# Modulation and gate products on four 32-column groups of TensorE, and a new order of work around the first value tiles

## What is computed

```python
def ada_terms(c, w_ada, b_ada):              # c: 2 rows in all, w_ada: 1024 x 3072
    m = jax.nn.silu(c) @ w_ada + b_ada
    shift, scale, gate = jnp.split(m, 3, axis=-1)

def project(x, c, norm_g, w_ada, b_ada, w_in, b_f):
    h = rmsnorm(x, norm_g) * (1.0 + scale[:, None, :]) + shift[:, None, :]
    p = h @ w_in                             # 1024 -> q, k, v, ag, logf, u, pg
    ...
def merge(x, attn, ag, pool, pg, gate, w_out):
    z = jnp.concatenate([attn * jax.nn.silu(ag), pool * jax.nn.silu(pg)], axis=-1)
    return x + gate[:, None, :] * (z @ w_out)
```

## Time and profile before

| | us |
|---|---|
| median of three runs | 1312.25 |
| the profiled execution, its own time | 1314.26 |
| its span in the trace | 1312.5 |
| PE busy | 1265.6 (96%) |
| DVE, ACT, POOL busy | 712.4, 564.3, 180.5 |

### The profile page before, as it was taken

How to read it: one execution, slowest core, us unless ns; L and a number is a source line. 1 busy time by engine, 2 the same in 40 slices (tenths; PEclk the granted TensorE clock), 3 DMA queues, 4 the chain that set the end, 5 groups by cost and what they waited for, 6 DMA issues and landing times. The chain is left out here.

```text
span 1312.5 us, 19345 instructions
## 1 busy us (share of the span) xinstructions
PE 1265.6 (96%) x7007; PEld 1038.7 (79%) x7007; DVE 712.4 (54%) x1965; ACT 564.3 (43%) x1158; POOL 180.5 (14%) x193
## 2 busy tenths in 40 slices
PE   7899999999999999999969999999999998999997
PEld 1669988888888888888848777877877876788885
DVE  0636631344456221110029999999999989544444
ACT  2536531221121212111128887887878878111111
POOL 1223310100100010100000031122104105100000
PEclk9899999999999999999979999999999999999999
DMA  9636444221221443432148849968786986766662
GB/s 367 244 121 190 157 142 140 77 89 42 67 88 43 135 145 125 140 117 83 49 135 162 117 77 169 129 116 147 85 149 116 128 169 158 208 204 193 192 193 64
DMA packets 163836, 179.51 MB, mean 137 GB/s; under 512 B 35361, under 2 KB 125013, under 8 KB 159974
## 3 DMA queue, kind: packets, MB, share of 16 engines
q1 hardware_dynamic: 158478, 160.42, 49.5%
q10 hardware_dynamic: 5264, 17.86, 4.2%
HBM read 111.55 MB, written 66.69 MB: 136 GB/s over the span
## 5 line engine op out<-in xcount | busy, mean ns | idle before, releaser
L597 PE MATMUL prj_acc<-prj_hhi,til_whi 128*128 128x512 f32 (+1 forms) x800 | 286.4, 358 | 0.0
L598 PE MATMUL prj_acc<-prj_hhi,til_wlo 128*128 128x512 f32 (+1 forms) x800 | 284.2, 355 | 0.0
L599 PE MATMUL prj_acc<-prj_hlo,til_whi 128*128 128x512 f32 (+1 forms) x800 | 284.2, 355 | 0.0
L1588 DVE TENSOR_SCALAR_CACHE_REDUCE att_wts<-att_sps 128x512 f32<-128x512 f32 (+4 forms) x328 | 186.3, 596 | 105.3 <-PE att_sps L1475 99.9
L1598 DVE TENSOR_TENSOR att_wlo<-att_tps,att_whi 128x512 fp32r<-128x512 f32 (+1 forms) x336 | 183.1, 583 | 20.8 <-ACT att_whi L1551 20.1
L1551 ACT ACTIVATE att_whi<-att_tps 128x512 fp32r<-128x512 f32 (+1 forms) x336 | 161.5, 515 | 57.7 <-PE att_tps L1488 25.4
L1545 ACT ACTIVATE att_wts<-att_wts,att_nm 128x1024 f32<-128x1024 f32 (+8 forms) x200 | 175.2, 880 | 20.4 <-DVE att_nm L1593 18.6
L1488 PE MATMUL att_tps<-keep_ident,att_wts 128*128 128x128 f32 x1088 | 159.0, 277 | 9.8 <-DVE att_wlo L1598 7.7
L599 PEld LDWEIGHTS prj_acc<-prj_hlo,til_whi 128*128 128x128 f32 x800 | 150.8, 188 | 21.3
L597 PEld LDWEIGHTS prj_acc<-prj_hhi,til_whi 128*128 128x128 f32 x800 | 150.8, 188 | 21.0
L598 PEld LDWEIGHTS prj_acc<-prj_hhi,til_wlo 128*128 128x128 f32 x800 | 150.8, 188 | 20.8
(11 more groups left out here) (181 smaller groups left out, 1857.0 us busy)
## 6 DMA issues: line engine op xcount, KB each, us to landing
til_wraw<-in_w_in SPq DMA_DIRECT2D x20, 512.0 KB, 4.3
scratch_v<-val_vs SPq DMA_DIRECT2D x17, 512.0 KB, 4.7
val_xt<-in_x_prompt ACTq DMA_DIRECT2D x16, 512.0 KB, 4.4
ini_al<-in_w_ada SPq DMA_DIRECT2D x8, 1024.0 KB, 15.8
zin_zh<-scratch_z SPq DMA_DIRECT2D x16, 512.0 KB, 4.3
zin_zl<-scratch_z SPq DMA_DIRECT2D x16, 512.0 KB, 5.8
zin_xr<-in_x_prompt SPq DMA_DIRECT2D x16, 512.0 KB, 5.4
out_y_prompt<-zin_o ACTq DMA_DIRECT2D x16, 512.0 KB, 2.7
```

The source lines that it names most:

```text
L597: pe.matmul(out, w[0][:, k, :], hhi[:, k, cs], start=(k == 0), stop=False)
L598: pe.matmul(out, w[1][:, k, :], hhi[:, k, cs], start=False, stop=False)
L599: mm = pe.matmul(out, w[0][:, k, :], hlo[:, k, cs], start=False, stop=(k == KT - 1))
L1588: dve.tensor_scalar(weights(st, x.row, x.w0, x.n), sps[x.i % S_RING][0:x.m, 0:x.n], 1.0, None, ALU.mult, ALU.max, accum_out=top[0:x.m, e, ...
```

## The change

Four things are done.

1. The four products of a slab go to different 32-column groups of PE's array: the output of block n lies on PSUM partitions 32n and 32n + 1 instead of 0 and 1 (`QUAD`), still one bank for each n. The gate's columns are cut into four blocks of 256 with k outside, and go to the four groups in the same way. The rows that are made of them (`mrow`, `gate_b`, `grow`) lie on the same partitions; the gate's bias comes in four DMAs instead of one and the gate leaves in four.
2. turn(0) and turn(1) stand between the slabs, after slab 4 and slab 6, instead of around the turning of `mrow`.
3. On ACT, square(3) and root(3), the copies of `mrow` and norm(2) stand ahead of the rounding of the value weights, and high(0) after its first half. On DVE, stats(3) stands ahead of the copies, and the low halves of the value weights after modulate(0). The value weights are loaded to other columns of `ah`, so SP waits for `turned` ahead of them.
4. value(t) runs through all k-blocks of high x high, then of high x low, then of low x high, and waits for the low half of the rows only ahead of the third; for tile 0 it waits for the weights block by block.

```diff
-        vraw = ah[:, :, 0:VC]
-        mrow = al[0:2, 0, 0:2 * D]
-        grow = ah[0:2, 0, D:2 * D]
+        vraw = ah[:, :, D - VC:D]
+        QUAD = [slice(32 * n, 32 * n + 2) for n in range(4)]
+        mrow = [al[QUAD[n], 0, n * 512:(n + 1) * 512] for n in range(4)]
+        grow = [ah[QUAD[n], 0, D + n * 256:D + (n + 1) * 256] for n in range(4)]
...
                 sp.dma_start(slab[:, k, :], wada[:, k, 0:2 * D]).then_inc(ada_in[k], 16)
+            sp.wait_ge(turned, 1)
...
             def gate():
-                for n in range(2):
-                    for k in range(KT):
-                        mm = pe.matmul(xps[GATE_SLOT][0:2, n * 512:(n + 1) * 512], pair[:, k, :], graw[:, k, n * 512:(n + 1) * 512],
+                for k in range(KT):
+                    for n in range(4):
+                        cs = slice(n * 256, (n + 1) * 256)
+                        mm = pe.matmul(xps[GATE_SLOT][QUAD[n], cs], pair[:, k, :], graw[:, k, cs],
                                        start=(k == 0), stop=(k == KT - 1))
...
             def value(t):
-                pe.wait_ge(lo_ok, t + 1)
+                pe.wait_ge(hi_ok, t + 1)
...
-                for k in range(KT):
-                    if t == 0:
-                        pe.wait_ge(w_lo, k + 1)
-                    for h, w in ((hhi, vhi_w), (hhi, vlo_w), (hlo, vhi_w)):
+                for h, w, split in ((hhi, vhi_w, w_hi), (hhi, vlo_w, w_lo), (hlo, vhi_w, w_lo)):
+                    if h is hlo:
+                        pe.wait_ge(lo_ok, t + 1)
+                    for k in range(KT):
+                        if t == 0:
+                            pe.wait_ge(split, k + 1 if h is hhi else KT)
...
                 for n in range(4):
-                    mm = pe.matmul(ada[n][0:2, :], pair[:, k, :], slab[:, k, n * 512:(n + 1) * 512],
+                    mm = pe.matmul(ada[n][QUAD[n], :], pair[:, k, :], slab[:, k, n * 512:(n + 1) * 512],
                                    start=(k == 0), stop=(k == KT - 1))
+                if k in (4, 6):
+                    turn((k - 4) // 2)
             mm.then_inc(m_full, 1)
-            turn(0)
             pe.wait_ge(m_row, 4)
...
-            turn(1)
...
-            square(2)
-            root(2)
+            for t in range(2, 4):
+                square(t)
+                root(t)
+            act.wait_ge(m_full, 1)
+            for n in range(2):
+                act.activation(mrow[n], ada[n][QUAD[n], :], ACT.Copy).then_inc(m_row, 1)
+            norm(2)
             for k in range(KT):
                 if k % 4 == 0:
                     act.wait_ge(vw_in[k // 4], 48)
+                if k == 4:
+                    high(0)
                 act.activation(vhi_w[:, k, :], vraw[:, k, :], ACT.Copy).then_inc(w_hi, 1)
-            act.wait_ge(m_full, 1)
-            for n in range(2):
-                act.activation(mrow[:, n * 512:(n + 1) * 512], ada[n][0:2, :], ACT.Copy).then_inc(m_row, 1)
-            norm(2)
-            square(3)
-            root(3)
-            high(0)
```

More of the change, by code:

```diff
@@ L268, in stage_project @@
         graw = ah[:, :, D:2 * D]
-        vraw = ah[:, :, 0:VC]
-        mrow = al[0:2, 0, 0:2 * D]
-        grow = ah[0:2, 0, D:2 * D]
-        gate_b = al[0:2, 1, D:2 * D]
+        vraw = ah[:, :, D - VC:D]
+        QUAD = [slice(32 * n, 32 * n + 2) for n in range(4)]
+        mrow = [al[QUAD[n], 0, n * 512:(n + 1) * 512] for n in range(4)]
+        grow = [ah[QUAD[n], 0, D + n * 256:D + (n + 1) * 256] for n in range(4)]
+        gate_b = [al[QUAD[n], 1, D + n * 256:D + (n + 1) * 256] for n in range(4)]
         pair = sc[:, :].rearrange("p (w k) -> p k w", w=2)
@@ L410, in _ @@
             sp.wait_ge(m_full, 1)
-            sp.dma_start(gate_b, io["b_ada"][:, 2 * D:].partition_broadcast(2)).then_inc(gb_in, 16)
+            for n in range(4):
+                bias = io["b_ada"][:, 2 * D + n * 256:2 * D + (n + 1) * 256]
+                sp.dma_start(gate_b[n], bias.partition_broadcast(2)).then_inc(gb_in, 16)
             b = v_slot(-1)
@@ L416, in _ @@
                 if t == GATE_AT:
-                    sp.wait_ge(g_ok, 2)
-                    sp.dma_start(dram["gate"][:, :], grow).then_inc(g_out, 16)
+                    for n in range(4):
+                        sp.wait_ge(g_ok, n + 1)
+                        sp.dma_start(dram["gate"][:, n * 256:(n + 1) * 256], grow[n]).then_inc(g_out, 16)
                 if t == NT - 2:
@@ L477, in _ @@
             store_chunk(sp, TILE_CHUNKS[-1])
-            sp.wait_ge(g_out, 16)
+            sp.wait_ge(g_out, 64)
             sp.wait_ge(f_out, 16 * 22)
@@ L524, in turn @@
                 elif t == GATE_AT + 3:
-                    pe.wait_ge(g_ok, 2)
+                    pe.wait_ge(g_ok, 4)
                 elif t >= 2:
@@ L680, in high @@
                 if t == KT:
-                    act.wait_ge(g_out, 16)
+                    act.wait_ge(g_out, 64)
                 act.activation(hhi[:, :, t * P:t * P + n], hf[:, t % 2, :].rearrange("p (k c) -> p k c", k=KT)[:, :, 0:n],
@@ L884, in _ @@
             dve.tensor_scalar(one_b[:, :], cols[:, ROW_B + KT:ROW_B + 2 * KT], 1.0, None, ALU.add).then_inc(ab, 1)
-            stats(0)
-            stats(1)
-            stats(2)
+            for t in range(4):
+                stats(t)
+            dve.wait_ge(m_full, 1)
+            for n in range(2, 4):
+                dve.tensor_copy(mrow[n], ada[n][QUAD[n], :]).then_inc(m_row, 1)
+            dve.wait_ge(ab, 1)
+            dve.wait_ge(m_col, 1)
+            wide = [P, KT, 2]
+            for n, (dst, bias) in enumerate(((keep["scale"], one_b[:, :]), (keep["shift"], cols[:, ROW_B:ROW_B + KT]))):
+                for q in range(2):
+                    ks = slice(4 * q, 4 * q + 4)
+                    dve.tensor_tensor(dst[:, ks, :], ada[2 - 2 * n + q][:, 0:KT].rearrange("p (k w) -> p k w", w=2),
+                                      bias[:, ks].unsqueeze(2).broadcast_to([P, 4, 2]), ALU.add).then_inc(ab, 1)
+            dve.wait_ge(ab, 5)
+            dve.tensor_tensor(keep["scale"][:, :, :], keep["scale"][:, :, :],
+                              cols[:, ROW_G:ROW_G + KT].unsqueeze(2).broadcast_to(wide), ALU.mult).then_inc(ab, 1)
+            dve.wait_ge(ab, 6)
+            modulate(0)
             for k in range(KT):
@@ L890, in _ @@
                 dve.tensor_tensor(vlo_w[:, k, :], vraw[:, k, :], raw(vhi_w[:, k, :]), ALU.subtract).then_inc(w_lo, 1)
[L891 to L906, removed]
             modulate(1)
@@ L913, in _ @@
                     dve.wait_ge(g_full, 1)
[L914 to L917, removed]
+                    dve.wait_ge(gb_in, 64)
+                    for n in range(4):
+                        dve.tensor_tensor(grow[n], xps[GATE_SLOT][QUAD[n], n * 256:(n + 1) * 256], gate_b[n], ALU.add).then_inc(g_ok, 1)
                 if t + 4 < NT:
```

3 lines of the change are left out of this document (2 added, 1 removed).

## The result

The changed kernel takes 1288.86 us (median of four runs, 1286.42 to 1289.4), the kernel before on the same chip 1311.82 (1310.92 to 1313.6): ratio 0.9825, interval 0.9809 to 0.984, 23.0 us less. The prediction was 1297.5 with a range of 1290 to 1304: the right sign, and too small a gain. The execution that was profiled lasted 1289.40 us.

What follows compares the result with a forecast made beforehand. PE was taken as the bound, busy 1265.6 of 1312.5 us. Gains of 8.5 us at the start and 6.2 at the gate, 14.7 together, brought the median from 1312.25 to a forecast of 1297.5 us, range 1290 to 1304.

Steps and rivals of the forecast that it cites:

- What bounds the start and that the rest follows: Start of the projection: PE ends the slab stage, not the DMA; what is gained ahead moves the whole packed remainder.
- I take this pairwise overlap: Slabs and gate: one product's second instruction runs beside the next product's first; slab 2.1 us, gate gain 6.2; chance 0.45.
- full-overlap rival: Slabs and gate: matmuls run four at a time; slab 1 us, gate 3.6 us, time 1292.3; chance 0.27.
- The clock between slabs: Rival at the slabs: PE's waits lower the clock; slab 3.4 to 4 us, start gains 4, time 1302; chance 0.10.
- M at 32.6: End of the slab products, called M: slab 7 done at 32.6 us, after turn(1) ends at 30.3; before, 39.7.
- value(0) starts at M + 8.3: Chain behind the slabs: copies, turning, modulate(0) and turn(2) take 8.3 us; first value product at 40.9 instead of 49.43.
- Clock up at 46.8: In value(0): PE's pace doubles at 46.8 us, taken between 44.9 and 48.7; turn(3) then at 49.3.
- POOL's 2.35 us beside the high products: Start: POOL's low half takes 2.35 us beside the products of the high half, which need only `hi_ok`.
- The sum: Whole kernel: 8.5 us gained at the start plus 6.2 at the gate, 14.7 us; the rest 0.

Runs made afterwards that it cites:

- e4: The changed kernel with the gate's four column blocks on two groups, issued 0, 0, 1, 1, slabs still on four; one run, 1294.45 us.
- e3: The changed kernel with the gate's four column blocks on two groups, issued 0, 1, 0, 1, slabs still on four; one run, 1305.35 us.
- e7: The changed kernel with turn(0) and turn(1) back behind the slab products instead of between them; 1290.42 us.
- e1: The changed kernel with all slab and gate products back on the first column group, new order of work kept; 1312.61 us.
- e9: The changed kernel with ACT's eight roundings of the value weights again ahead of its copies, norm(2) and high(0); 1296.99 us.
- e10: The changed kernel with DVE's modulate(1) ahead of the last four low weights and value(0)'s low x high part ahead of high x low; 1293.03 us.

## Why the prediction was wrong, step by step

- **What bounds the start and that the rest follows**: right. What is gained by the end of the gate, 22.15 us, is the difference of the medians (23.0) within 1 us; the two profiled executions lie 24.9 apart.
- **"I take this pairwise overlap"**: this step failed, in the slabs and in the gate. I let the second instruction of a product hold up the next product, as if matmuls began in program order. They ran four at a time: a slab in 1.04 us, not 2.1 to 2.3, the gate in 3.56, not 7.6. e4 is the direct evidence against the order, e3 with the four-group rows for groups that run independently. My full-overlap rival had the mechanism and both prices (1 us a slab, 3.6 us the gate, gains 9.7 and 10.2) at a chance of 0.27; nothing in the rows of before favored the pairs, and the argument rested on an assumption about order that no row bore out.
- **The clock between slabs**: it did fall (0.71 over 14.2 to 38.7), as that rival had it. A slab then takes 1.89 us, still less than the 2.86 between two, and the last slab ran at the upper level, so here it cost nothing. It can cost something: in e7 the last slab ran at the lower level, and the copies came 0.76 us later. I had priced a slab at the lower level at 3.4 to 4 us, with the pairs.
- **M at 32.6**: it was 31.2. PE was done with turn(1) at 29.8 and waited 0.33 us for slab 7, then took 1.04 us for it.
- **"value(0) starts at M + 8.3"**: M + 7.2. The turning of the rows took 0.45 us instead of 1.14, a second overlap that I missed, and turn(2)'s start to value(0) took 1.60, not 1.94.
- **Clock up at 46.8**: the stretches of 4 us show 0.55 for 38 to 42 and 1.00 from 42 on, and the products change pace at 41.8, 5.0 us after turn(2)'s start. value(0) took 7.5 us for my 8.4.
- **POOL's 2.35 us beside the high products**: it took 5.90 and was ready at 43.75, 0.06 us before PE used it. The step held only by that, which was luck: I had not looked at what DVE does beside POOL.
- **The sum**: start 12.0 for 8.5 (M 1.4, chain 1.1, value(0) 0.9), gate 10.3 for 6.2; together 7.6 us missing. The median came 8.6 below my 1297.5, the other 1.0 lying behind the gate. The full-overlap rival's 1292.3 lacks 2.3 us of the start (9.7 for 12.0) and about 1 behind the gate.

## What to carry to other kernels

Small products that fill few columns of the array are worth spreading over its column groups even in float32, and their time here went by the number of products on a group, not by the order of issue (all groups had equally many; uneven ones weren't run). Before pricing such a change, ask of each wait behind it whether the work ahead of it on the other engines still has its cover: here the groups alone gained 0.85 us at the start and the order alone, its two turns ahead of the last slab included, nothing, together 12. When two rules for an overlap are open and no row decides, give them like chances, and price the smaller operations of the same kind too.

## What the runs showed of the hardware

- **Column groups run independently** (with equally many products on each): the gate's 64 instructions took 13.90 us to the next turn on one group (e1), 7.01 on two in either order, 3.56 on four. The Trainium skill ("TensorE: Matmul & The Clock Gate", Part 3, what overlaps and what doesn't) has matmuls in strict order of start and end; e4's 7.01 us disagree with that for this form, and its measured 2.38 times for three column tiles lies below what these rows give, 3.9 for four.
- **Row groups too**: the 16 turnings of `mrow` took 0.45 us from four row groups (0.62 in e9, at a granted clock of 0.50), from one 1.15 (e1).
- **POOL and DVE hold each other up.** POOL's 2.35 us became 5.90 beside DVE's subtractions of two SBUF operands (36.53 to 41.50), and ended 2.25 us after them; in e10 it ended 2.27 us after the first four (38.90). It went the other way as well: in e10 a DVE copy of 128x8 took 2.37 us instead of the changed kernel's 0.17 and ended at 46.84, with POOL's piece (46.82). The Trainium skill ("SBUF — State Buffer", Who interferes with whom) says that a VectorE instruction with two SBUF inputs and a GpSimd instruction that reads SBUF exclude each other; the rows of the subtractions agree. The copy of 128x8 has one input, so that sentence does not cover it.
